# Gate and up products of the small experts in two column tiles of 64

## What is computed

```python
gate = jnp.minimum(xb @ w_gate[e] + b_gate[e], SWIGLU_LIMIT)
up = jnp.clip(xb @ w_up[e] + b_up[e], -SWIGLU_LIMIT, SWIGLU_LIMIT)
act = gate * jax.nn.sigmoid(SWIGLU_ALPHA * gate) * (up + 1.0)
y = act @ w_down[e] + b_down[e]
```

## Time and profile before

| | us |
|---|---|
| median of 3 runs | 2073.2 (2072.0 to 2074.21) |
| span of the profiled execution | 2073.2 |
| PE busy with matmuls | 2011.8 (97%) |
| PE busy with weight loads | 1643.8 (79%) |
| VectorE busy | 655.5 (32%) |
| ScalarE busy | 283.8 (14%) |
| GpSimd busy | 232.9 (11%) |
| DMA, mean over the span | 242 GB/s |

### The profile page before, as it was taken

The page is one execution under the profiler, slowest core; times in us unless marked ns, Lnnn a source line. Parts: engine busy times, 40 slices in busy tenths (PEclk is TensorE's granted clock), DMA queues, the critical chain, the costliest instruction groups (busy, mean ns, idle before and its releaser), DMA issues.

```text
span 2073.2 us, 32125 instructions
## 1 busy us (share of the span) xinstructions
PE 2011.8 (97%) x13457; PEld 1643.8 (79%) x13458; DVE 655.5 (32%) x1363; ACT 283.8 (14%) x457; POOL 232.9 (11%) x381
## 2 busy tenths in 40 slices
PE   8999988996999999999999999999999999999996
PEld 4444455554998898889788999988888888989996
DVE  3115676443223222222222332222222222222223
ACT  2001245111011001101001010111010100100103
POOL 0001333212000001000001010010000000000103
PEclk9999999997999999999999999999999999999998
DMA  4210022214878879998999988899899998887855
GB/s 173 81 41 1 1 92 84 100 61 152 305 248 305 307 272 322 321 329 296 321 322 318 309 294 272 286 319 335 312 304 322 319 319 310 279 299 260 287 189 199
DMA packets 231449, 500.89 MB, mean 242 GB/s; under 512 B 7766, under 2 KB 8303, under 8 KB 231298
## 3 DMA queue, kind: packets, MB, share of 16 engines
q1 hardware_dynamic: 218880, 454.46, 61.0%
q0 software_dynamic: 12368, 44.26, 8.6%
q10 hardware_dynamic: 50, 0.01, 0.0%
HBM read 463.63 MB, written 35.13 MB: 241 GB/s over the span
## 4 chain that ended last, share of the span: by engine, by line
PE 72%; DMA 1%; DVE 1%; issue 1%; SPq 0%; ACT 0%; POOL 0%; POOLq 0%; DVEq 0%; ACTq 0%
PE ps L1694 57%; PE ps L1721 12%; PE ps L1708 2%; PE ps L1714 1%; PE ps L1701 1%; DMA qk<-x_rows 1%; DMA out<-qk 0%; DVE x L1254 0%; DMA hT<-h_rows,hT 0%; DMA x_rows<-x,hT 0%; DVE qk L1363 0%; SPq L439 0%; DVE xn L1221 0%; ACT hT L821 0%; ACT x L857 0%
## 5 line engine op out<-in xcount | busy, mean ns | idle before, releaser
L1694 PE MATMUL ps<-hT,qk 128*128 128x128 f32 (+8 forms) x4096 | 501.7, 284 | 6.8 <-issue 6.8
L1694 PEld LDWEIGHTS ps<-hT,qk 128*128 128x128 f32 x4096 | 493.5, 192 | 16.6 <-issue 16.0
L1721 PE MATMUL ps<-w_ring,hT 128*128 128x512 f32 x576 | 251.8, 593 | 0.0
L1694 PE MATMUL ps<-hT,u_all 128*128 128x128 f32 (+8 forms) x2048 | 247.7, 282 | 0.0
L1694 PE MATMUL ps<-hT,v 128*128 128x128 f32 (+8 forms) x2048 | 247.7, 282 | 0.0
L1694 PEld LDWEIGHTS ps<-hT,v 128*128 128x128 f32 x2048 | 244.6, 191 | 0.0
L1694 PEld LDWEIGHTS ps<-hT,u_all 128*128 128x128 f32 x2048 | 244.6, 191 | 0.0
L1694 PE MATMUL ps<-hT,w_ring 128*128 128x132 f32 (+7 forms) x1792 | 233.8, 291 | 5.0 <-DVE x L1254 3.6
L1694 PEld LDWEIGHTS ps<-hT,w_ring 128*128 128x128 f32 x1792 | 229.3, 190 | 7.4 <-issue 7.0
L1721 PEld LDWEIGHTS ps<-w_ring,hT 128*128 128x128 f32 x576 | 107.5, 190 | 126.7 <-issue 126.3
L558 POOL DMA_INDIRECT hT<-h_rows,hT x46 | 45.3, 986 | 1148.9 <-issue 672.1
(11 more groups left out here) (250 smaller groups left out, 1470.6 us busy)
## 6 DMA issues: line engine op xcount, KB each, us to landing
w_ring<-in_w_down SPq DMA_DIRECT2D x64, 2048.0 KB, 7.9
qk<-in_w_gate SPq DMA_DIRECT2D x32, 2048.0 KB
qk<-in_w_up SPq DMA_DIRECT2D x32, 2048.0 KB
v<-in_w_gate SPq DMA_DIRECT2D x32, 2048.0 KB, 10.5
u_all<-in_w_up SPq DMA_DIRECT2D x32, 2048.0 KB, 8.7
x<-in_b_down SPq DMA_DIRECT2D x32, 512.0 KB, 11.6
w_ring<-in_w_in SPq DMA_DIRECT2D x3, 2048.0 KB, 9.0
x<-in_x SPq DMA_DIRECT2D x8, 512.0 KB, 12.4
```

The source lines that it names most:

```text
L1694: ins = pe.matmul(bank[:, m, 0:n], w[g][:, k, m * P:(m + 1) * P], rhs[:, k, 0:n], start=k == 0, stop=k == KC - 1)
L1721: ins = pe.matmul(ps[:, 2 * (g % PAIRS), :], aT[:, k, 0:P], w[g][:, k, :], start=k == 0, stop=k == KC - 1)
```

## The change

Four things. The widths become 96, 108, 120, 128, 136, 144, 152, 160, 168, 180 and 192 (132, 140 and 148 are gone). The border between one block and two is no longer index 0 but the index of 128 (`ONE_BLOCK`, 3). In an expert of one block the groups 0 to 3 go through the new `half_columns`: each product of 128 weight columns becomes two of 64, whose results go to PSUM partitions 0 to 63 and 64 to 127. And those products move 96, 108, 120 or 128 columns instead of 128 always. Down of these experts still goes through `rows_of` with 128 rows, and VectorE still reads 128 columns.

```diff
-WIDTHS = (128, 132, 136, 140, 144, 148, 152, 160, 168, 180, 192)
+WIDTHS = (96, 108, 120, 128, 136, 144, 152, 160, 168, 180, 192)
+ONE_BLOCK = WIDTHS.index(P)
...
-            with eng.If(wide > 0):
+            with eng.If(wide > ONE_BLOCK):
                 body(2)
             with eng.Else():
                 body(1)
...
+                def half_columns(bank, g, n, rhs, tiles):
+
+                    for m, k in tiles:
+                        for c in range(2):
+                            part = slice(c * P // 2, (c + 1) * P // 2)
+                            ins = pe.matmul(bank[part, m, 0:n], w[g][:, k, m * P + part.start:m * P + part.stop], rhs[:, k, 0:n],
+                                            start=k == 0, stop=k == KC - 1)
+                    return ins
...
                 def expert(i, n):
                     e = nc.snap(e_reg, min_val=0, max_val=E - 1)
+                    two_blocks = i > ONE_BLOCK
 
                     def product(g, rhs, tiles=whole):
-                        return columns(pair[g % PAIRS], g, n, rhs, tiles)
+                        return (columns if two_blocks else half_columns)(pair[g % PAIRS], g, n, rhs, tiles)
...
-                    if i:
+                    if two_blocks:
                         product(4, aT, early)
                     else:
                         rows_of(4, range(KC // 2))
...
-                    with pe.If(after > 0):
+                    with pe.If(after > ONE_BLOCK):
...
-                            call(hints, after, 1, len(WIDTHS) - 1)
+                            call(hints, after, ONE_BLOCK + 1, len(WIDTHS) - 1)
...
-                        call(hints, after, 0, 0)
+                        call(hints, after, 0, ONE_BLOCK)
...
-                    (product(5, aT) if i else rows_of(5, range(KC))).then_inc(group_done, 1)
-                    pe.reg_mov(before, int(i > 0))
+                    (product(5, aT) if two_blocks else rows_of(5, range(KC))).then_inc(group_done, 1)
+                    pe.reg_mov(before, int(two_blocks))
```

More of the change, by code:

```diff
@@ L832, in back @@
                     wide = width_of(act, e)
-                    with act.If(wide > 0):
+                    with act.If(wide > ONE_BLOCK):
                         for h, n in enumerate(HALVES):
@@ L1724, in turn_second @@
                 def turn_second(e, wide):
-                    with pe.If(wide > 0):
+                    with pe.If(wide > ONE_BLOCK):
                         pe.wait_ge(xT_ready, 2 * e + 1)
@@ L1822, in expert @@
                     pe.sem_inc(passed, 1)
-                    (product(4, aT, late) if i else rows_of(4, range(KC // 2, KC))).then_inc(group_done, 1)
+                    (product(4, aT, late) if two_blocks else rows_of(4, range(KC // 2, KC))).then_inc(group_done, 1)
                     hints = {}
-                    with pe.If(after > 0):
+                    with pe.If(after > ONE_BLOCK):
                         with pe.If(after > len(WIDTHS) - 1):
@@ L1866, in _ @@
                 nc.switch_bb("experts_end", parent=start)
-                with pe.If(width_of(pe, E - 1) > 0):
+                with pe.If(width_of(pe, E - 1) > ONE_BLOCK):
                     pe.wait_ge(y_ready, 2 * E)
```

## The result

The changed kernel takes 2043.6 us (median of 4 runs, 2042.9 to 2044.7) against 2073.3 us (2072.0 to 2074.2): a ratio of 0.986, with an interval of 0.985 to 0.987. That is 29.7 us less, where 38.8 were forecast; the forecast was 2034.4 in a range of 2016 to 2070.

The account below looks back on a forecast made before the run. PE was taken as the bound, busy 97% of the span, mostly in column products limited by weight loads. 2073.2 - 54.9 + 5.1 + 9.0 + 2 = 2034.4 us, range 2016 to 2070.

Parts of the forecast that it names:

- The product: Gate and up of 18 small experts: 165, 185, 205 or 218.3 ns a product against 223.2, 54.9 us gained.
- rival 1: Two column tiles' weight loads don't overlap: 234 ns a product at any width, 2114 us, slower; chance 0.12.
- rival 2: A weight load doesn't overlap the other tile's matmul: 276 to 329 ns a product, about 2290 us; chance 0.04.
- rival 3: Column tiles don't run side by side at all: 330 to 437 ns a product, about 2494 us; chance 0.03.
- rival 5: Change does nothing, steps staying at 111.6 ns: 2089 us, chance 0.01; or small costs eat the gain: near 2073, chance 0.02.
- The wide widths: Four wide experts move four columns more, 132 to 136 or 140 to 144: 1.27 us each, 5.1 us lost.
- The switches: PE's changes between tiled and untiled work at edges of groups: 9.0 us lost, between 0 and 15.
- PE's queue: Twice the instructions per product, so queued work lasts half as long and index work may show: 2 us, between 0 and 10.
- rival 4: PE waits for instructions, fetched pieces partly uncovered in 18 small experts: +29 us, 2063 us; chance 0.08.
- The clock: PE's granted clock should stay at full speed, 2.4 GHz; no cost was given.
- VectorE: VectorE's work per group is unchanged; its last three operations after group 3, about 2 us, stay hidden.
- DMA: Weight loads need at least 36 us an expert, the shortest new expert has 36.7 us, so they stay hidden.

Follow-up runs that it names:

- the widths alone: The changed kernel with its new widths, but small experts' gate and up products go through the untiled product of 128 weight columns: 2080.5 us, ratio 1.004.
- the kernel with one body of 96 columns: The changed kernel with one body for all small experts, gate and up moving only 96 columns (tokens 97 to 128 left out): 1961.5 us, ratio 0.946.
- the kernels with four tiles: The changed kernel with small experts' products in four column tiles of 32: 2328.6 us; the same with one body of 128 columns: 2336.8 us.

## Why the prediction was right, and where not

*The product.* Right, to the nanosecond: 165, 205 and 218.4 ns at 96, 120 and 128 columns against 165, 205 and 218.3, where PE is neither starved nor at a lower clock. That a load of 128 columns was the bound was shown by the widths alone, which bring nothing. That two column tiles work as the two row tiles of the earlier trace rows did was the step with the least behind it, and it held. Rivals 1, 2, 3 and 5 fall together with that: groups start 5.3 to 7.0 us apart as their columns ask, up to 7.2 with a switch between, and the few above that (7.7 to 7.9 us) hold idle time or a fall of the clock. The rule of the Trainium skill ("TensorE: Matmul & The Clock Gate", Part 3), that a load overlaps only matmuls of another row group, doesn't hold here: both tiles use all rows, and four loads beside four matmuls take 205.0 ns. (The same part also lets a load into a background weight buffer go ahead of matmuls; this measurement doesn't contradict that.)

*The wide widths.* Right: 0.21 us a group more at 136 and at 144, x 6 x 4 = 5.0 us; putting the widths back gave 4.6 us.

*The switches.* 9.0 us in the forecast, 8.3 read from the groups: +0.17 us into group 0 (0.15), -0.07 for group 1, where the index's own switch goes (-0.08), +0.14 to 0.18 before the transposes (0.20), and 0.61 for two `back` steps (0.68).

*The supply of instructions.* This term was sized wrong: 2 us, between 0 and 10, under "PE's queue". The span is 2042.4, so the rest of the sum is 2042.4 - 2073.2 + 54.9 - 5.1 - 8.3 = 10.7 us. From the groups' times, 5.5 us of it are lost inside bodies for want of instructions (3.7 in expert 22, 0.9 in expert 10, 0.6 in expert 17, 0.3 in experts of 120 columns), and about 3.6 at the jumps into experts 1 and 21. The forecast had the mechanism as rival 4, with a chance of 0.08, and priced it at 29 us by taking every piece as partly uncovered. What it costs depends on how fast PE asks. At 128 columns PE wants an instruction every 27.3 ns and loses nothing inside a body; at 120 every 25.6 ns, and loses little in the change, though up to 1.2 us in a group in its variants; at 96 every 20.6 ns, and three groups of fresh bodies lose 0.6 to 2.4 us each. Only 3 experts are at 96 and 3 at 108, so most of rival 4's price isn't paid. So the forecast's own case and rival 4 are both true, each in its place. The stalls at jumps come with the new set of bodies, and the forecast had no term for them beyond its 2 us.

*The clock.* The forecast said that it stays at 2.4 GHz and gave it no price. It fell twice to 1.2 GHz, each time behind idle time of PE that the change had brought, and cost 3.2 us.

*Group 1 ahead of a wide expert.* In experts 7, 12, 19 and 25, each the last small one ahead of an expert of two blocks, group 1 loses 0.3 us, 1.1 in all, in short gaps always behind some 92 of its 128 matmuls. No piece is being fetched then (none between 1395 and 1412, expert 19), and the kernel with one body of 96 columns loses 0.9 us at the like places, in repeated bodies too, where none is either. So this is not the fetching of code; its cause is open.

*VectorE.* The forecast said that nothing changes there. 1.7 us came from it: the index of expert 3 waits 2.2 us for L1222, where 0.5 us were waited before. The views of an expert in the middle of the run, on which the forecast rested, don't show it, since the lists are made once only. Against that, the step from `turn_in(1)` to group 5 in experts 0, 13, 14 and 15 takes 1.8 us less in all, since VectorE's L1255 holds it less (0.75 to 0.85 us each before, at most 0.44 after). It does so in the kernel of the widths alone too, so it has nothing to do with the tiles; no step of the forecast had it.

*What helped by chance.* The first group of expert 0 starts 1.0 us earlier, behind a part that the change doesn't touch; the clock rises a little earlier in that group (0.4 us); and several small differences, 0.5 of it at the jump out of expert 8, come to 0.9.

Together: 5.5 + 3.6 + 3.2 + 1.1 + 1.7 - 1.8 - 1.0 - 0.4 - 0.9 = 11.0, for the 10.7 us that were to be explained. So the main term was right, and the total came as near as it did since some 4 us that nobody had forecast went the other way.

*DMA.* Right, and nearer the edge than the page of the changed kernel lets one think: the 2 MB loads land later (into `w_ring` after 8.8 us instead of 7.9, into `v` 11.6 instead of 10.5, into `u_all` 9.9 instead of 8.7), and no matmul of an expert waits for weights.

What stays open: why the same jump stalls in one layout of the bodies and not in another, what the gaps in group 1 are, and whether the pieces come at their own pace or are asked for late. For the latter speaks that one of the two pieces in expert 22 begins only as PE runs dry, and that in the kernels with four tiles some begin 3.6 us apart.

## What to carry to other kernels

When a stream of matmuls is bound by its weight loads, narrower operands bring nothing until the loads are cut too; column tiles do that, if the tiles alternate matmul by matmul. Count instructions as well as columns: unrolled code that isn't repeated came at some 23 ns an instruction, and what asks for more (two tiles at 96 columns, four tiles at any) waits. Before adding a specialised body, ask how often it runs twice in a row: here the narrowest width saves 7.7 us on paper and 0.2 us in the three experts that use it, and the kernel without it is some 4 us faster, for a stall at a jump and a fall of the clock. Count an idle time of PE with what follows it: behind two of 2.2 and 2.8 us the clock fell and cost 1.6 us more each time. And look at the clock by short stretches, not by the row of 40 slices.

## What the runs showed of the hardware

- A load of 128 columns in float32 takes 111.6 ns and bounds any product that moves fewer than some 131 columns ((111.6 - 2.5) / 0.833). Two tiles of 64 columns load and multiply side by side at 0.833 n + 2.5 ns a step, and four tiles of 32 at nearly the same (101 ns at 120 columns), as long as there are instructions and the clock is at 2.4 GHz.
- By the recorded starts a matmul may overtake those of another tile, by three or four (25 steps for 32 matmuls; one run).
- The granted clock fell from 2.4 to 1.2 GHz for 3.4 us behind 2.2 and 2.8 us of idle time of PE in a stream that was busy before it, and groups in it took 1.4 to 1.7 us more. The idle times of 1.1 and 2.1 us in expert 22 were followed by no fall. With four tiles it fell 40 times, for 154 us in all.
- Code is fetched in pieces of 16 KB, in about 1 us of DMA time. Where bodies of 128 columns are entered anew the trace has 231 to 279 matmuls and loads between two pieces, 253 on average, so a piece is some 256 instructions. Where PE had run dry it went on 2.2 to 2.5 us after a piece's start. Where four tiles asked for more, fresh code came at some 23 ns an instruction on average. A repeated body of two tiles isn't fetched again and runs at 20.6 ns an instruction; one of over 130 KB is.
- The DMAs carried 378 GB/s over a whole expert, 13.99 MB in 37 us, with loads landing after 13 to 16 us, and PE didn't wait for them.
